# A hybrid decoder step in split fp32: who makes the low parts of the weights in the first part of the gated recurrence

## The reference

```python
h = rmsnorm(x, norm_mix)
q, k, v, g_ret, x_lru, y_lru, g_a, g_b = split(h @ w_in)          # D_MODEL 1024
ret_branch = (silu(g_ret) * group_norm(retention(rope(q), rope(k), v))) @ w_ret_out
xc = causal_conv(x_lru, conv_state, conv_w, conv_b)               # width 1280, 4 taps
r, i = sigmoid(xc @ blocks(w_a) + b_a), sigmoid(xc @ blocks(w_x) + b_x)   # 16 blocks of 80
a = exp(-8 * r * softplus(-lam))
hl = scan of  h_t = a_t * h_(t-1) + sqrt(1 - a_t**2) * (i_t * xc_t)
lru_branch = (gelu(y_lru) * hl) @ w_lru_out
x = x + (sigmoid(g_a + b0) * ret_branch + sigmoid(g_b + b1) * lru_branch) @ w_o
x = x + (silu(gate) * up) @ w_down                                # gate, up = rmsnorm(x) @ w_gate_up
```

## Time and profile before

| | us |
|---|---|
| median of the runs | 2475.91 |
| lowest, highest of 3 | 2473.72, 2479.89 |
| the profiled execution | 2477.37 |
| its span | 2475.6 |

### The profile page before, as it was taken

How to read it: one execution, slowest core, us unless ns; L and a number is a source line. 1 busy time by engine, 2 the same in 40 slices (tenths; PEclk the granted TensorE clock), 3 DMA queues, 4 the chain that set the end, 5 groups by cost and what they waited for, 6 DMA issues and landing times.

```text
span 2475.6 us, 53938 instructions
## 1 busy us (share of the span) xinstructions
PE 2432.7 (98%) x19636; PEld 2365.6 (96%) x19636; DVE 1177.9 (48%) x1587; ACT 645.5 (26%) x981; POOL 1633.5 (66%) x1685
## 2 busy tenths in 40 slices
PE   7999999999999999999999999999999999999997
PEld 7999999999999999999999999999999999999997
DVE  7645463679644532022266363636786454221223
ACT  2404040446721211011114040413666112100111
POOL 5464646477887776766755555555878777667764
PEclk9999999999999999999999999999999999999998
DMA  5636363522233322332247363635323322223222
GB/s 207 230 124 243 116 238 120 204 85 81 89 108 92 95 86 84 103 94 83 89 163 250 112 242 121 242 124 190 92 84 93 100 95 88 91 82 106 86 84 86
DMA packets 121748, 315.69 MB, mean 128 GB/s; under 512 B 12192, under 2 KB 12960, under 8 KB 121568
## 3 DMA queue, kind: packets, MB, share of 16 engines
q1 hardware_dynamic: 60480, 199.78, 25.8%
q10 hardware_dynamic: 61088, 113.34, 12.8%
HBM read 272.69 MB, written 40.38 MB: 126 GB/s over the span
## 4 chain that ended last, share of the span: by engine, by line
PE 91%; DVE 3%; ACT 2%; DVEq 2%; issue 1%; ACTq 0%; POOLq 0%; DMA 0%; POOL 0%
PE proj L366 55%; PE aux L366 27%; PE aux L619 2%; DVE scratch L1101 1%; PE aux L578 1%; PE aux L551 1%; PE proj L627 1%; PE aux L627 1%; DVEq L1104 1%; DVE scratch L1159 1%; PE aux L605 1%; PE proj L619 0%; ACT L1521 0%; DVEq L1162 0%; ACT L1527 0%
## 5 line engine op out<-in xcount | busy, mean ns | idle before, releaser
L354 POOL TENSOR_TENSOR w_low<-w_raw,w_high 128x512 fp32r<-128x512 f32 x840 | 1084.4, 1291 | 124.6 <-issue 2.7
L352 POOL TENSOR_SCALAR w_high<-w_raw 128x512 fp32r<-128x512 f32 x840 | 555.2, 661 | 693.2 <-PE proj L366 527.0
L366 PE MATMUL proj<-x_high,w_high 128*128 128x260 f32 x2752 | 561.2, 285 | 24.3 <-DVE x_low L775 14.3
L366 PE MATMUL proj<-x_high,w_low 128*128 128x260 f32 x2752 | 556.9, 284 | 0.0
L366 PE MATMUL proj<-x_low,w_high 128*128 128x260 f32 x2752 | 556.2, 284 | 0.0
L366 PEld LDWEIGHTS proj<-x_high,w_high 128*128 128x128 f32 x2752 | 426.9, 190 | 34.5 <-issue 18.9
L366 PEld LDWEIGHTS proj<-x_high,w_low 128*128 128x128 f32 x2752 | 426.7, 190 | 0.0
L366 PEld LDWEIGHTS proj<-x_low,w_high 128*128 128x128 f32 x2752 | 426.2, 190 | 0.0
L366 PE MATMUL proj<-split_scratch,w_high 128*128 128x260 f32 x2544 | 409.5, 283 | 0.0
L366 PEld LDWEIGHTS proj<-split_scratch,w_high 128*128 128x128 f32 x2544 | 348.8, 188 | 5.0 <-issue 5.0
L366 PE MATMUL aux<-x_high,w_high 128*128 128x260 f32 x1344 | 271.1, 283 | 0.0
(11 more groups left out here) (191 smaller groups left out, 2291.2 us busy)
## 6 DMA issues: line engine op xcount, KB each, us to landing
w_raw<-in_wstream SPq DMA_DIRECT2D x252, 512.0 KB, 3.5
scratch<-in_sret ACTq DMA_DIRECT2D x96, 512.0 KB, 6.8
out_ret_s<-scratch ACTq DMA_DIRECT2D x64, 512.0 KB, 4.2
w_raw<-in_wstream SPq DMA_DIRECT2D x72, 448.0 KB, 3.3
w_raw<-in_wstream SPq DMA_DIRECT2D x48, 384.0 KB, 3.0
scratch<-v_rows ACTq DMA_DIRECT2D x64, 256.0 KB, 4.0
w_raw<-in_wstream SPq DMA_DIRECT2D x48, 320.0 KB, 2.8
out_ret_p<-scratch ACTq DMA_DIRECT2D x8, 512.0 KB, 3.2
```

The costliest lines, as they stand in the source:

```text
L352: pool.tensor_scalar(WH[:, j, w], WR[:, j, w], 1.0, 0.0, ALU.mult, ALU.add)
L354: pool.tensor_tensor(WL[:, j, w], WR[:, j, w], WH[:, j, w].bitcast(F32), ALU.subtract).then_inc(s["w_split"], 1)
L366: m = pe.matmul(out, wt[:, w, blk * P:(blk + 1) * P], x[xi], start=first and n == 0, stop=last and n == 2)
```

## The change

In the first group, from the second unit of y(0,0) to x(1,4) (16 units per layer), POOL makes only the high parts, without a drain, and raises a new count, `w_high`, by one for each half. VectorE makes the low part of the whole unit in one subtraction (`weight_low`), when both halves of the high part are there, and raises `w_split` by two. The subtractions are put between VectorE's own operations. Before the first unit behind this stretch POOL waits for `w_split`, so that the counts come in order.

```diff
+V_FIRST, V_LAST = LRU_UNIT["y", 0, 0] + 1, LRU_UNIT["x", 1, 4]
+V_LOWS = V_LAST - V_FIRST + 1
...
@@ POOL
                                 if h == 0:
                                     pool.wait_ge(w_ld[j], ...
+                                if base + k == V_LAST + 1:
+                                    pool.wait_ge(s["w_split"], u + (h + 4))
                                 pool.sem_inc(s["go_pool"], 1)
+                                if times == 1 and V_FIRST <= base + k <= V_LAST:
+                                    pool.tensor_scalar(WH[:, j, w], WR[:, j, w], 1.0, 0.0, ALU.mult, ALU.add
+                                                       ).then_inc(s["w_high"], 1)
+                                    continue
                                 pool.tensor_scalar(WH[:, j, w], WR[:, j, w], 1.0, 0.0, ALU.mult, ALU.add)
                                 pool.drain()
                                 pool.tensor_tensor(WL[:, j, w], WR[:, j, w], WH[:, j, w].bitcast(F32),
...
@@ VectorE
+                def weight_low(*what, part=0):
+                    u = LRU_UNIT[what] + part
+                    n, j = LRU_SIZES[u - B_LRU], u % 2
+                    dve.wait_ge(s["w_high"], layer * (2 * V_LOWS) + 2 * (u - V_FIRST + 1))
+                    tt(WL[:, j, 0:n * P], WR[:, j, 0:n * P], WH[:, j, 0:n * P].bitcast(F32), ALU.subtract
+                       ).then_inc(s["w_split"], 2)
...
                 for t in range(GT):
                     conv_low(*((0, 2) if t == 0 else FILL_X[t - 1]))
+                    weight_low("y", 0, t, part=1)
                     gate_input(0, t)
+                    weight_low("x", *FILL_X[t])
                     read_y(0, t)
                     one_less_a2(0, t)
+                    if t < GT - 1:
+                        weight_low("y", 0, t + 1)
+                    else:
+                        weight_low("x", 1, 3)
                     read_x(*FILL_X[t])
                     scan(0, t)
                     conv(*FILL_X[t])
                     gated_low(0, t)
+                weight_low("x", 1, 4)
                 read_x(1, 3)
```

More of the change, by code:

```diff
@@ L248, in build @@
         AUX = ctx.enter_context(nc.psum_tensor("aux", [P, 4, 512], F32))
-        names = ("go_pool setup_ld boot w_split w_used p_done t_free r_done "
+        names = ("go_pool setup_ld boot w_high w_split w_used p_done t_free r_done "
                  "rope_done qk_high qk_low qz_full st_high st_low aux_mm kv_high kv_low "
```

## The result

| | before | after |
|---|---|---|
| median, us | 2474.72 | 2539.83 |
| lowest, highest | 2472.49, 2479.89 | 2539.62, 2541.25 |
| span of the profiled execution | 2475.6 | 2538.0 |

Five runs of each. The ratio is 1.0264, 95% interval 1.0253 to 1.0275: 65 us more, where 77 were predicted.

The account below looks back on a forecast made before the run. TensorE, busy 98% of the span, was taken as the bound. Per layer, stops of 34.0 us plus 9.0 for the clock minus 4.6 for the old stop made 38.4; two layers, +77, gave 2552 us, range 2520 to 2590.

Parts of the forecast that it names:

- The place decides: In VectorE's order the second unit's low parts follow read, scan, conv, gated_low and conv_low, so TensorE stops six times per layer.
- The chain from T: From TensorE's end of an x tile (T) to the second unit's low parts: 11.4 us (10.4 to 15.5).
- Read to scan: Chain term from VectorE's read of the x tile to the end of line 1164: 4.5 us, low end 4.1.
- Scan to high part: Chain term from the scan's end to the end of ScalarE's high part of the convolved tile: 4.5 us, low end 4.1.
- The port: VectorE operations with both inputs in SBUF take turns with POOL's high parts: possibly 1 to 2 us more per turn.
- The old stop: TensorE's 3.1 us stop at 608.9, waiting for an x tile's reader, goes with its clock loss: -4.6 us per layer.
- The clock: Each of six new stops per layer costs 1.5 us (0 to 3) in lower clock, 9.0 us per layer.
- Relief: Rival: VectorE, rid of POOL's subtractions, falls to about 13.5 us per turn and stops lagging; 2467 us, 3%.
- T + 5.05: When TensorE, 7 blocks after ending an x tile at T, needs the second unit's low parts; 5.05 in us.
- Stops without the clock: Rival: the stops come as worked out but the clock stays up, as TensorE works in between; 2534 us, 15%.
- The stretched chain: Rival: POOL's high parts disturb VectorE as much as both parts did, t = 1 to 4 stops grow; 2587 us, 12%.
- VectorE's turn would fit beside its new work: VectorE's work per turn shrinks to about 10 us; with 3.4 of subtractions it stays below TensorE's 15.87.

Follow-up runs that it names:

- Experiments 1: Kernel early: against the changed kernel, same 16 subtractions placed earlier, second units of y right behind the x-tile read; 2472.72 us, 0.9981 of the kernel before.
- 2: Against the kernel of experiment 1, the next unit's subtraction stands ahead of one_less_a2 instead of behind it; 2469.29 us, 0.9973 of the kernel before.
- 6: Against the changed kernel, the second unit's subtraction for t = 1 to 4 stands behind the previous turn's conv, ahead of gated_low; 2518.29 us, 1.0169 of before.
- 7: Kernel behind_scan: against the changed kernel, the second unit's subtraction for t = 1 to 4 stands behind the scan, ahead of conv; 2501.54 us, 1.0106 of before.
- load-only: Against the kernel before, POOL still makes both parts; VectorE adds 16 same-sized subtractions on other data, each after a drain, nobody waiting; 2504.11 us, 1.0106.
- pool_seconds: Against the changed kernel, the five second units of y(0,t) get low parts from POOL again, 11 of 16 subtractions stay on VectorE; 2490.10 us, 1.0049 of before.

## Why the prediction was right, and where it was off

- **The place decides.** Right. All twelve new waits end at the subtraction, six per layer, at the units named. Experiments 1, 2, 6 and 7 move only the place and go from 2540 to 2518, 2502, 2473 and 2469 us.
- **The chain from T.** Right in its steps, 9.6 us instead of 11.4. The mis-sized terms are the two long ones, both measured below their low ends of 4.1. Read to scan took 3.7 us instead of 4.5: the low end put only the scan at its shortest, but the small operation behind the scan fell too, from 0.51 us to the 0.14 of line 1179. It was in the turn of the kernel before:

```profile
536.40 0.51 DVE L1161 TENSOR_TENSOR scratch<-scratch 128x8 f32<-128x8 f32 x1
```

  Scan to high part took 3.9 instead of 4.5: ScalarE alone sets its end, as the taps are done 0.45 us before it is free, and the least that the prediction gave ScalarE, 4.1, was 0.2 too much. The waits were 23.6 us per layer (47.2 / 2), not 34.0: stops of 2.5, three of 4.4, 5.0 and 2.7 us instead of 3.2, three of 6.3, 7.0 and 4.9. The last is off by most, since its conv took 2.7 us instead of 3.7 besides.
- **The port.** The rule of the Trainium skill ("SBUF — State Buffer", section "SBUF: two separate sides") pointed to 1 to 2 us more per turn, if three of POOL's high parts met the chain. Only two met it, 1.5 us in all, and one of them beside the read from PSUM, which took its usual 0.70. The other, at 540.24, agrees with the rule in kind: it took 0.99 us instead of 0.62, and VectorE's operation on 8 columns that began at 540.66 ended with it, after 0.58 us. In the last turn, with no high part beside it, the same line took 0.16:

```profile
629.78 0.16 DVE L1116 TENSOR_TENSOR scratch<-scratch,conv_state_sum 128x8 f32<-128x8 f32 x1
```

  These 0.4 us cost TensorE nothing, since ScalarE was later than the taps anyway. What VectorE gains when POOL's subtractions are gone is worth 8 us in the run without low parts; that run does not tell the port from other causes.
- **The old stop.** Right: it is gone. Before, VectorE had fallen behind; now TensorE waits for it in every turn.
- **The clock.** Right in kind, too small in total. One lower stretch costs 1.5 us, as taken, and eleven of the twelve stops were followed by one; but behind four of the six stops of 4.4 us it lasted twice as long. The net cost was 21 to 23 us in both layers, where the sum had 2 x 7.5 = 15. Part of the shorter waits is thus given back.
- **The rivals.** Relief is real, 0.9961 at most, and 0.9973 was reached with the subtractions placed by the chain; as the change places them it failed at the point named, T + 5.05. Stops without the clock: refuted by the windows. The stretched chain: refuted by the 9.6 us of the chain and by line 1162. That VectorE's turn would fit beside its new work was right (12.7 us busy in the turn from 536.80 to 560.10, where 13.4 was worked out), and it is what made experiments 1 and 2 possible.

Sum by the measured terms, per layer: 23.6 - 2.9 + 11 = 31.7, two layers 63, against 62.4 in the spans. That the total came within 12 us of the forecast owes something to luck: the waits were 21 us below the sum in both layers, the clock 6 to 8 above it.

Open: why like stops are followed by a lower stretch in one layer and not in the other. That was seen, not explored.

## What to carry to other kernels

When an engine takes over a step of a pipeline with two buffers, adding up its work is not enough: draw the chain from the event that starts a turn to the moment its result is needed, with everything that stands ahead of it in the engine's order, its waits for other engines included. Put the new step directly behind the last event that it really needs, which here was worth 70 us at the same instructions. Then look for what is late next, since each step taken off one stop may uncover another.

## What the runs showed of the hardware

- VectorE's subtraction, undisturbed, took 0.95, 1.08 and 1.23 us for 768, 896 and 1024 columns, 1.1 ns per column, against POOL's mean of 1.39 us for 512.
- The same 896 columns beside POOL's subtractions took up to 2.01 us, in the timeline of the load-only kernel:

```profile
546.29 2.01 DVE L1102 TENSOR_TENSOR trig<-residual 128x896 f32<-128x896 f32 x1
...
553.75 1.22 DVE L1102 TENSOR_TENSOR trig<-residual 128x896 f32<-128x896 f32 x1
```

- In this stage stops of TensorE of 1.1 to 1.8 us left the clock at full (kernels early, pool_seconds and behind_scan); stops of 2.2 to 2.9 us were followed by its lower level in some cases only, and those of 4.4 us and more always, by 3.4 or 6.8 us of it. In the windows after the stop that ended at 546.4 TensorE ran 33 matmuls in 6.8 us where 57 would fit at 0.118:

```profile
546.40:553.20 6.80, 6.77 (x33) 6.77 (x34) 1.81 (x2) 2.96 (x4) 1.24 (x2) 0.55 0.43 136
```
